# Layer 0's shift and scale taken by quarters, x transposed ahead, and the first chunk projected between the loads

## The reference, cut to what matters

```python
shift, scale, gate = split(silu(c) @ ada_w[0] + ada_b[0], 3)        # ada_w[0]: 2048 x 6144; the same for c_ctx
h  = rmsnorm(x,   norm_w[0]) * (1 + scale)   + shift                # 256 x 2048
hc = rmsnorm(ctx, norm_w[0]) * (1 + scale_c) + shift_c
q, k, v, g = split(t @ gla_w_in)                 # t = h and hc; gla_w_in: 2048 x 6144
log_a[d] = log_sigmoid((t @ gate_a1[d]) @ gate_a2[d] + gate_b[d]) / 16      # d = 0, 1; rank 16
```

## Time and profile before

| | |
|---|---|
| median of the runs | 1828.95 us |
| span of the profiled execution | 1822.9 us |
| what lies around it, from the median | 6.0 us |
| TensorE busy | 1711.7 us, 94% |
| VectorE / ScalarE busy | 908.2 us (50%) / 553.2 us (30%) |
| DMA | 265.54 MB, mean 146 GB/s |

### The profile page before, as it was taken

One profiled execution on the slowest core, in us unless ns is written; L12 is line 12 of the kernel. 1 busy time (PEld: TensorE's weight loads), 2 busy tenths in 40 slices (PEclk: granted clock), 3 DMA queues, 4 the chain that ended last, 5 costly groups with the idle time before them and its releaser, 6 DMA issues.

```text
span 1822.9 us, 19640 instructions
## 1 busy us (share of the span) xinstructions
PE 1711.7 (94%) x7996; PEld 1276.2 (70%) x7996; DVE 908.2 (50%) x1523; ACT 553.2 (30%) x805; POOL 2.2 (0%) x9
## 2 busy tenths in 40 slices
PE   3869999999999999989999799999999999997798
PEld 0237687778678777857777577877787787776476
DVE  0126544354353426455333457575565756557564
ACT  1222333233333323333222323242332323233142
POOL 0000000000000000000000000000000000000000
PEclk9579999999999999999999899999999999999799
DMA  8975422453344245223555326244433524423063
GB/s 316 386 279 174 146 86 73 160 173 93 105 154 141 88 144 178 83 81 130 194 173 190 115 78 224 93 139 136 153 127 116 185 81 133 158 93 124 14 194 118
DMA packets 185582, 265.54 MB, mean 146 GB/s; under 512 B 16090, under 2 KB 99988, under 8 KB 184980
## 3 DMA queue, kind: packets, MB, share of 16 engines
q1 hardware_dynamic: 180660, 256.68, 42.8%
q10 hardware_dynamic: 4832, 7.60, 1.4%
HBM read 262.14 MB, written 2.10 MB: 145 GB/s over the span
## 4 chain that ended last, share of the span: by engine, by line
PE 86%; DVE 5%; DMA 4%; SPq 2%; ACT 1%; issue 1%; ACTq 0%; DVEq 0%
PE bank L716 70%; PE bank L677 4%; DMA w_raw<-in_ada_w 4%; PE bank L838 2%; PE bank L787 2%; PE bank L930 2%; PE bank L914 2%; PE bank L735 1%; SPq L317 1%; PE bank L783 1%; DVE w_lo L971 1%; PE bank L685 1%; ACT w_hi L434 1%; DVE work L1251 1%; DVE work L1054 1%
## 5 line engine op out<-in xcount | busy, mean ns | idle before, releaser
L716 PE MATMUL bank<-w_lo,acts_hi 128*128 128x512 f32 x1664 | 667.1, 401 | 15.1 <-DVE acts_lo L1077 7.2
L716 PE MATMUL bank<-w_hi,acts_lo 128*128 128x512 f32 x1664 | 649.8, 391 | 0.0
L716 PE MATMUL bank<-w_hi,acts_hi 128*128 128x512 f32 x1664 | 649.5, 390 | 0.0
L971 DVE TENSOR_TENSOR w_lo<-w_raw,w_hi 128x1024 fp32r<-128x1024 f32 x288 | 351.6, 1223 | 478.6 <-ACT w_hi L434 478.4
L434 ACT ACTIVATE w_hi<-w_raw 128x1024 fp32r<-128x1024 f32 x288 | 303.9, 1058 | 897.0 <-PE bank L716 877.0
L716 PEld LDWEIGHTS bank<-w_lo,acts_hi 128*128 128x128 f32 x1664 | 313.1, 188 | 126.8 <-issue 38.2
L716 PEld LDWEIGHTS bank<-w_hi,acts_lo 128*128 128x128 f32 x1664 | 313.0, 188 | 67.1
L716 PEld LDWEIGHTS bank<-w_hi,acts_hi 128*128 128x128 f32 x1664 | 313.5, 188 | 62.4 <-issue 1.7
L677 PE MATMUL bank<-ada_w,silu_p 128*32 128x512 f32 x640 | 98.8, 693 | 24.3 <-DMA ada_w<-in_ada_w 24.3
L716 PE MATMUL bank<-acts_hi,w_lo 128*128 128x512 f32 x256 | 104.1, 407 | 10.3 <-DVE acts_lo L1077 10.3
L716 PE MATMUL bank<-acts_lo,w_hi 128*128 128x512 f32 x256 | 100.3, 392 | 0.0
(11 more groups left out here) (150 smaller groups left out, 1181.5 us busy)
## 6 DMA issues: line engine op xcount, KB each, us to landing
ada_w<-in_ada_w SPq DMA_DIRECT2D x80, 1024.0 KB, 7.6
w_raw<-in_diff_w_in SPq DMA_DIRECT2D x256, 256.0 KB, 3.0
w_raw<-in_gla_w_in SPq DMA_DIRECT2D x192, 256.0 KB, 3.0
w_raw<-in_ada_w SPq DMA_DIRECT2D x16, 1024.0 KB, 9.2
w_raw<-in_gla_w_out SPq DMA_DIRECT2D x64, 256.0 KB, 3.4
w_raw<-in_diff_w_out SPq DMA_DIRECT2D x64, 256.0 KB, 3.5
u<-in_x SPq DMA_DIRECT2D x2, 1024.0 KB, 13.9
u<-in_ctx SPq DMA_DIRECT2D x2, 1024.0 KB, 16.5
```

Of the source, the lines that this page charges most:

```text
L716: last = pe.matmul(bank[t][:], a, b, start=(k == 0 and i == 0), stop=(k == NK - 1 and i == 2))
L971: dve.tensor_tensor(w_lo[:, p % RING], raw[:, p % RING], w_hi[:, p % RING].bitcast(F32), ALU.subtract)\
```

## The change

**Loads.** x and ctx are issued first, the vectors, constants and `gate_a1` from ScalarE's queue, the last in one transfer with 8 KB rows, which TensorE turns by 16 small transposes. The startup quads come in the order shift 0, scale 0, shift 1, scale 1 and so on (`startup_chunk`), so that each group of eight completes four k-tiles. Quads 0 to 7 use three slots; from quad 8 on there are six, four of them in the space of x and ctx, so quads 8 to 11 wait for the last transpose (`xt_ok`). The pairs of chunk 0 are loaded two with each group of eight quads.

**x ahead.** Squares, norm and the 16 transposes come before modulation: VectorE copies the even transposed tiles out of their bank, ScalarE the odd, to `xT` in SBUF.

**By quarters.** With each two blocks taken, VectorE scales and shifts four k-tiles of `xT` in place, ScalarE rounds them, VectorE takes the remainders. TensorE projects two pairs of chunk 0 and 8 of the gate columns' 32 matmuls (four k-tiles) for each quarter, between the quads of the next.

**Background quads.** None is left in chunk 0: the first four go behind pairs 8 to 11, the next behind 21 to 24, the next behind 26 to 29 (before: 0, 1, 3, 5; 7, 8, 10, 11; 24, 25, 27, 29).

The core of the diff, without the empty lines, the new names of semaphores and the moved small loads:

```diff
     i, q = m // 4, m % 4
+    if i < 3:
+        return ((8, 9, 10, 11), (21, 22, 23, 24), (26, 27, 28, 29))[i][q]
     if i < 2 * G_HEADS:
         return 3 * (i // 2) * PAIRS + ((7, 8, 10, 11) if i % 2 else (0, 1, 3, 5))[q]
     if i < 2 * G_HEADS + 4:
         return (OUT0 + i - 2 * G_HEADS) * PAIRS + (0, 1, 3, 5)[q]
     return (DIFF + 4 * (i - 2 * G_HEADS - 4)) * PAIRS + (5, 7, PAIRS + 2, PAIRS + 5)[q]
+def startup_chunk(i):
+    return i // 2 + 4 * (i % 2)
+def startup_slot(n):
+    if n < 8:
+        return n % 3, n // 3
+    r, s = (n - 8) // 6, (n - 8) % 6
+    return (3 + s, r) if s < 4 else (s - 4, 3 + r)
+ADA_USES = 7
...
+        xT = view(0, NK, TOK)
+        x_sq = view(0, NT, D)
+        a1_raw = work[0:2 * NK, NT * D:NT * D + P * G_RANK].rearrange("e (p r) -> e p r", r=G_RANK)
...
-        quad_slot = [ada_w[:, 0], ada_w[:, 1], raw_quads[:, 0:4], raw_quads[:, 4:8]]
-        vec1 = view(9728, P)
-        vec2 = view(9856, P)
-        lam_pr = view(9984, 2)
+        u_quads = u[:].rearrange("p t (j n) -> p t j n", n=CW)
+        quad_slot = [ada_w[:, 0], ada_w[:, 1], raw_quads[:, 4:8]] + [u_quads[:, t] for t in range(NT)]
...
             def startup_quad(n):
-                if n >= 4:
-                    sp.wait_ge(ada_used, n - 3)
-                a, q = n // 4, n % 4
-                sp.dma_start(quad_slot[n % 4], aw0[:, 4 * q:4 * q + 4, a * CW:(a + 1) * CW]).then_inc(ada_in[n % 4], 16)
+                slot, _ = startup_slot(n)
+                if 3 <= n < 8:
+                    sp.wait_ge(ada_used, n - 2)
+                elif 8 <= n < 12:
+                    sp.wait_ge(xt_ok, NK)
+                elif n >= 12:
+                    sp.wait_ge(ada_used, n - 5)
+                a, q = startup_chunk(n // 4), n % 4
+                sp.dma_start(quad_slot[slot], aw0[:, 4 * q:4 * q + 4, a * CW:(a + 1) * CW]).then_inc(ada_in[slot], 16)
...
+            def first_chunk(q):
+                late = q == 3
+                for n in range(8 * q, 8 * q + (7 if late else 6)):
+                    startup_quad(n)
+                load_pair(0, 2 * q, q_and_k(0))
+                for n in range(8 * q + (7 if late else 6), 8 * q + 8):
+                    startup_quad(n)
+                load_pair(0, 2 * q + 1, q_and_k(0))
+            for q in range(4):
+                first_chunk(q)
...
+            def columns_out(ks):
+                for k in ks:
+                    act.wait_ge(xt_ok, k + 1)
+                    act.activation(xT[:, k], bank[5][:], ACT.Copy).then_inc(xT_odd, 1)
+            row_squares()
+            rsqrt(1, NT)
+            act.wait_ge(sq_ok, NT)
+            columns_out((1, 3))
             modulation_rows(0)
-            act.wait_ge(a1_in, 32)
-            act.activation(a1[:, NK], a1_raw[:, 0:2], ACT.Copy)
-            act.activation(a1[:, 0:NK, 0], a1_raw, ACT.Copy).then_inc(a1_hi_ok, 1)
-            modulation_rows(1)
-            act.wait_ge(x_in, 16 * NT)
-            row_squares()
-            modulation_rows(2)
-            rsqrt(1, NT)
-            for a in range(3, STARTUP):
-                modulation_rows(a)
-            splits(0, range(4))
-            high_parts(0, hf, 0)
+            columns_out(range(5, NK, 2))
+            act.wait_ge(a1_t, 1)
+            act.activation(a1[:, NK], ones[:, 0:4 * G_RANK].rearrange("p (a r) -> p a r", a=2), ACT.Copy)
+            act.activation(a1[:, 0:NK, 0].rearrange("p k (d r) -> p k d r", d=2),
+                           bank[5][:].rearrange("p (r d k) -> p k d r", r=G_RANK, d=2), ACT.Copy).then_inc(a1_hi_ok, 1)
+            for q in range(4):
+                if q > 0:
+                    modulation_rows(2 * q)
+                modulation_rows(2 * q + 1)
+                split(0, 2 * q)
+                for k in range(4 * q, 4 * q + 4):
+                    act.wait_ge(hf_ok, k + 1)
+                    act.activation(hi[:, k, :], xT[:, k], ACT.Copy).then_inc(hi_ok, 1)
+                    if k % 4 == 1:
+                        split(0, 2 * q + 1)
...
-                pe.wait_ge(ada_in[slot], 16 * (n // 4 + 1) if n < QUADS else 16 * (STARTUP + (n - QUADS) // 2 + 1))
+                pe.wait_ge(ada_in[slot], 16 * (1 + (startup_slot(n)[1] if n < QUADS else ADA_USES + (n - QUADS) // 2)))
+                if n == QUADS + 4:
+                    pe.wait_ge(d2_ok, 1)
...
+            def startup_quads(first, last):
+                for n in range(first, last):
+                    ada_quad(n, startup_slot(n)[0], bank[6 + n // 4 % 2])
+            def startup_sum(i):
+                modulation_sum(i, bank[6 + i % 2])
+            def row_transposes(k0):
+                for k in range(k0, k0 + 4):
+                    if k > 1:
+                        pe.wait_ge((xT_even, xT_odd)[k % 2], k // 2)
+                    for t in range(NT):
+                        last = pe.transpose(bank[4 + k % 2][:, t * P:(t + 1) * P], u[:, t, k * P:(k + 1) * P], ident[:])
+                    last.then_inc(xt_ok, 1)
+            def gate_weight_transposes():
+                pe.wait_ge(a1_in, 16)
+                pe.wait_ge(xT_odd, NK // 2)
+                for r in range(G_RANK):
+                    last = pe.transpose(bank[5][:, r * 2 * NK:(r + 1) * 2 * NK], a1_raw[:, :, r],
+                                        ident[0:2 * NK, 0:2 * NK])
+                last.then_inc(a1_t, 1)
+            def first_pair(p):
+                pe.wait_ge(acts_ok, 2 * p + 2)
+                project_pair(0, p, NT, False)
+            def gate_columns(q):
+                if q == 0:
+                    pe.wait_ge(a1_ok, 1)
+                    pe.wait_ge(xT_even, NK // 2)
                 columns = a1[:].rearrange("p k a r -> p (k a r)")
-                for k in range(NK):
+                for k in range(4 * q, 4 * q + 4):
                     w = columns[:, k * 4 * G_RANK:k * 4 * G_RANK + P]
                     pe.matmul(bank[4][:], w, hi[:, k, :], start=(k == 0), stop=False)
                     last = pe.matmul(bank[4][:], w, lo[:, k, :], start=False, stop=(k == NK - 1))
-                last.then_inc(z_ok, 1)
-                pe.wait_ge(zT_ok, 1)
+                if q == 3:
+                    last.then_inc(z_ok, 1)
+                    pe.wait_ge(zT_ok, 1)
+            startup_quads(0, 4)
+            pe.wait_ge(xn_ok, NT)
+            row_transposes(0)
+            startup_quads(4, 5)
+            startup_sum(0)
+            row_transposes(4)
+            startup_quads(5, 6)
+            row_transposes(8)
+            startup_quads(6, 7)
+            row_transposes(12)
+            gate_weight_transposes()
+            startup_quads(7, 9)
+            startup_sum(1)
+            for q in range(3):
+                n = 8 * (q + 1)
+                startup_quads(n + 1, n + 2)
+                first_pair(2 * q)
+                startup_quads(n + 2, n + 4)
+                first_pair(2 * q + 1)
+                startup_quads(n + 4, n + 5)
+                startup_sum(2 * q + 2)
+                gate_columns(q)
+                startup_quads(n + 5, min(n + 9, QUADS))
+                startup_sum(2 * q + 3)
+            first_pair(6)
+            first_pair(7)
+            gate_columns(3)
...
-            gla_head(0, before=transposing(0, xn), gates=gate_columns)
-            for h in range(1, G_HEADS):
+            for h in range(G_HEADS):
...
-            take_modulation(0, 0, 0, bank[6])
-            dve.wait_ge(a1_hi_ok, 1)
-            dve.tensor_tensor(a1[:, 0:NK, 1], a1_raw, a1[:, 0:NK, 0].bitcast(F32), ALU.subtract).then_inc(a1_ok, 1)
-            take_modulation(1, 0, 4, bank[7])
             dve.wait_ge(sq_ok, NT)
             inverse_rms(1, NT, D)
-            row_norm(range(NT))
-            for a in range(2, STARTUP):
-                take_modulation(a, 0, 4 * a, bank[6 + a % 2])
-            scale_columns(0, STARTUP)
...
-            dve.wait_ge(xn_ok, NT)
-            activation_tiles(0, hf, modulated(0), 0)
+            def columns_out(ks):
+                for k in ks:
+                    dve.wait_ge(xt_ok, k + 1)
+                    dve.tensor_copy(xT[:, k], bank[4][:]).then_inc(xT_even, 1)
+            def first_remainder(k):
+                dve.wait_ge(hi_ok, k + 1)
+                dve.tensor_tensor(lo[:, k, :], xT[:, k], hi[:, k, :].bitcast(F32), ALU.subtract).then_inc(acts_ok, 1)
+            def first_quarter(q):
+                for i in (2 * q, 2 * q + 1):
+                    a = startup_chunk(i)
+                    take_modulation(i, 0, 4 * a, bank[6 + i % 2])
+                dve.wait_ge(ada_taken, 2 * q + 2)
+                s = mod[:, 1, 4 * q:4 * q + 4]
+                w = cols1[:, V_NORM + 4 * q:V_NORM + 4 * q + 4].unsqueeze(2).broadcast_to([P, 4, 2])
+                st.step(dve.scalar_tensor_tensor(s, s, 1.0, w, ALU.add, ALU.mult))
+                st.wait()
+                emit = modulated(0)
+                for k in range(4 * q, 4 * q + 4):
+                    dve.wait_ge((xT_even, xT_odd)[k % 2], k // 2 + 1)
```

(72 more changed lines are left out.)

99 lines of the change are left out of this document (45 added, 54 removed).

## The result

The changed kernel took 1811.05 us (median of 4 runs, 1809.72 to 1813.36) against 1827.11 (4 runs) of the kernel before beside it: ratio 0.9914, 95% interval 0.9893 to 0.9935. It is faster by 16.1 us, where 27.1 were forecast; the time is 9.2 us above the forecast and inside the range. The profiled span went from 1822.9 to 1807.9 us, 15.0 less.

What follows compares the result with a forecast made beforehand. DMA was taken to bound the first stretch (quad loads), PE the last. 190.64 - 155.2 - 5.8 - 2.5 = 27.1 us gained: span 1795.8, with 6.0 added time 1801.9 us; range 1786 to 1819.

Steps and rivals of the forecast that it cites:

- The bound: Start of the old kernel: DMA bounds the quad loads, PE the work after; moving that work into the loads gains time.
- the mark: End of chunk 0's gate columns (start of the first gate_zT copy): 190.64 us before, forecast 155.2, 35.4 earlier.
- Term 1, DMA: Loads before the mark: 40 quads' worth at 2.71 us, 108.4 us of a full queue, with DMA running ahead of PE.
- The first rival: In the quarters DMA is the bound at 24.4 us each; gain 41.5 us, time 1787.4; chance 0.17.
- Term 2, the start: From the launch through norm, transposes and first quads: last transpose at about 45, sum 1 ends at 53.9 us.
- all at the fast rate 47.7: Lower bound for the end of sum 1 if all PE work in the start runs at the fast rate: 47.7 us.
- The fourth rival: The start takes longer through the held quads, sum 1 at 58.7 or later: gain 22 or less, 1807; no separate chance.
- Term 3, a quarter: Each quarter after an odd sum: PE's serial list with a 4.8 us chain, 27.6 us against DMA's 24.4; last quarter 18.8.
- pair 6.7: First pair of each quarter, behind a 3.8 us PE pause: starts slow and takes 6.7 us, against 5.5 at speed.
- No loss of clock: PE holds the fast level through the pause, first pairs take 5.5 instead of 6.7: the time 5 us less.
- The two rivals in which the clock stayed low for quads and small matmuls too: In the quarters: partly low, 1823 (half of that 1812), chance 0.20; low throughout, 1834.4, chance 0.06 with the like.
- Term 4, given back: Behind the mark: 5.8 us for moved background quads and a sum, 2.5 us waiting for a quad after pair 10.

Runs made afterwards that it cites:

- gates_last: Changed kernel with all 32 gate-column matmuls behind pair 7 of chunk 0 instead of a quarter at a time; ratio 0.9902 to the kernel before, 1812.01 us.
- three_quads: Changed kernel with all three free quads of a quarter put into the pause before its first pair, instead of one; ratio 0.9862 to the kernel before, 1801.57 us.
- transposes_together: all_five with all 16 transposes in one run behind quad 4, so quads 8 to 11 are issued sooner; ratio 0.9764 to the kernel before, 1783.00 us.
- all_five: Changed kernel with squares_first, pair_11, three_quads and remainder_first together, plus 15 filler matmuls in the last quarter's pause; ratio 0.9777, 1785.62 us.
- squares_first: Changed kernel with ACT's row squares ahead of its SiLU, which waits for a constant; ratio 0.9868 to the kernel before, 1803.36 us.
- remainder_first: Changed kernel with each quarter's first weight remainder made while the sum still runs, not between the tiles; ratio 0.9875 to the kernel before, 1807.28 us.
- busy_fit: Changed kernel with 6, 15, 15 and 20 useless PE matmuls filling the pauses before the four first pairs; ratio 0.9858 to the kernel before, 1799.28 us.
- pair_11: Changed kernel with the third background quad of chunk 1 one pair later, behind pair 11; ratio 0.9887 to the kernel before, 1808.61 us.
- busy_pause: Changed kernel with 12, 26, 26 and 32 useless PE matmuls in the pauses before the four first pairs; ratio 0.9885 to the kernel before, 1808.31 us.

## Why the prediction was right, and by how much it was not

**The bound (right).** DMA bounded the old start and PE did too little beside it; the change took 25.9 us off the mark. In the kernel before, 65.3 us of PE's work (125.34 to 190.64) followed the loads; now 14.9 us follow the last pause (149.88 to 164.78). No run takes the parts of the change apart, so how much each gave is not shown. Of one part the traces give a size: the gate weights, in pieces of 16 floats, kept the 16 DMA engines as full as large loads do but at half the rate in 28 to 33 us of the kernel before (first line); the kernel after moved large loads there (second line). That is 5 x (1 - 187 / 376) = 2.5 us of load, by estimate, and that is no large share of the 25.9.

```profile
28.00:33.00 5.00, 0.00 (x0) 0.00 (x0) 0.00 (x0) 0.78 (x2) 0.00 (x0) 1.00 1.01 187
```

```profile
28.00:33.00 5.00, 0.85 (x4) 0.00 (x0) 4.65 (x8) 0.18 (x1) 0.00 (x0) 1.00 1.06 376
```

**Term 1, DMA (right).** 40 quads' worth could run ahead of PE: in the changed kernel PE waited 0.6 us for DMA in 30 to 160 us, and gates_last lengthened sum 1 to mark by 1.5 us, not 5.5. The first rival (1787.4) did not come; but it stood only some 3 us a quarter away, as 27.6 against 24.4 says: three_quads waits for DMA in each of its first three quarters, and transposes_together runs two of them in 24.4 and 24.5.

**Term 2, the start (mis-sized: 53.9, measured 58.3).** The step that failed is "ACT's 13 small issues [...] hold ACT until about 6.5, hidden: it would only wait for x". Their issue was hidden; their landing wasn't. The squares stood behind SiLU in ACT's order, and SiLU behind a constant that landed at 17.3, so that they began at 19.84 and not at 11 to 12. The landing of the constants issued on ACT's queue (line 477) in the kernel after (before, line 282: 1.8 to 1.9 us):

```profile
DMA to landing us min/median/max: 9.4/10.0/11.2
```

The last transpose ended at 49.3 for 45; with the squares first, sum 1 was at 53.55, which is the forecast's 53.9. Part of that hit is luck. In squares_first the transposes began at 29.08, behind quad 3, and not at 27; they and the quads between them then took 15.3 us and not 17.7, as most of them ran at the fast pace (a quad 1.00, a sum 1.05) where the slow one was priced (1.76, 1.80). (The lower bound "all at the fast rate 47.7" comes out at 48.8 by its own terms, four quads at 1.0 and two sums at 0.8; nothing rests on it.) The fourth rival, a longer start with sum 1 at 58.7, so came in its number (58.3), but not through the held quads that it named. The held quads idled DMA as forecast: a share of 0.37 over 13 us (37 to 50) is 8.2 us without load, for 7. In the changed kernel that cost PE little, as it had other work until 53.9 and waited 0.6 us; in the versions that DMA bounds it is a price in full: transposes_together issues them 4.0 us sooner than all_five and has the mark 4.2 sooner.

**Term 3, a quarter (the order right, one price off).** The chain came out at 4.8 us exactly (87.47 to 92.29), by luck, as errors cancel: a tile took 0.65 to 0.73, not 0.5, but the takes cost 0.4 and not 0.6, and a remainder 0.60 in the chain and not 0.68. Behind it 4 quads took 3.57, not 4.0. What was mis-sized is the first pair ("pair 6.7"): 8.30, 7.36 and 8.56. The row of 7.08 that I leaned on was behind a longer pause, and I took the shorter to cost less. The runs don't show that: behind 10.3 us of idle the row was 7.08, behind 3.0 and 3.9 (the changed kernel) 8.30, 7.36 and 8.56, behind 2.0 and 2.9 (remainder_first) still 7.70, 7.36 and 7.35. Behind one and the same pause of 3.9 us it was 7.1 to 8.6 over the kernels. busy_fit measured the price with everything else in place: 1.6 to 2.8 us a quarter. No loss of clock, which I had priced at 5 us, is worth 8.1 to 9.0.

For the clock the row was 1.93 against 1.07 for a quad. The pairs now show it too: 8.30 us at a granted clock of 0.67, begun slow and ended fast, against 5.73 at 1.00 behind fillers. The Trainium skill ("TensorE: Matmul & The Clock Gate", "What's actually happening") says that the lower clock is the default and that activity lifts it. By that rule matmuls of no use in a pause should pay, and busy_fit agrees, with 8.1 to 9.0 us.

The two rivals in which the clock stayed low for quads and small matmuls too (1812 to 1823, and 1834.4) did not come: in the quarters quads took 0.9 to 1.0 and sums 0.98 to 1.07, but for the quad right behind sum 1 (1.93), which the chain through DVE covers. Their near end, 1812, lies by the measured time, but by other terms.

**Term 4, given back (mis-sized: 8.3, measured 12.6).** The wait for the quad behind pair 10 came where it was put, at 2.95 us for 2.5. It also cost some 1.7 us of slower work behind it, which was not in the sum at all, though the same price stood in term 3. Of the other 2.6 the wait's own length is 0.45 and 0.2 could not be placed. From chunk 1's pair 13 to the gate logits of head 1 it was 5.6 us more for 4 quads and a sum, which I had at 4.8: a pair behind a quad took 5.67, not 5.45. Some 1.1 us lie further on and were not traced to a place.

**The sum of the misses** at layer 1's norm is 4.4 + 4.3 + 0.9 + 4.3 = 13.9 us, less 1.7 that the rest ran faster: the span is 12.1 above the forecast 1795.8. That the time is only 9.2 above its forecast is luck: the 6.0 us added to the span were 3.1 in the changed kernel (1811.05 less 1807.9). What stays open: why the constants land so late. They are issued at 4.6 to 6.6 us, while x, ctx and the first quads fill the 16 engines (a DMA share of 1.04 in 3 to 8 us, against 0.35 in the kernel before); that those hold them up was not tried by itself.

## To carry to other kernels

When work is moved beside a stream of loads, write PE's program out as a serial list per stage and look for the spot where it waits for another engine: what stands there decides, and independent work of the same length belongs exactly in that spot. Price a pause of PE at its length plus what the matmuls behind it lose by the clock (here 1.6 to 2.8 us on 3 to 5 us, and still 1.6 to 2.0 on 2 to 3 us), and if there is no work for it, matmuls of no use that end just before the pause does are better than nothing, while ones that outlast it give the gain back. A small load that has moved behind large ones must be priced by its landing, and everything queued behind its waiter with it.

## What the runs showed of the hardware

- Loads of 1 to 64 KB, issued on ACT's queue while x and 1 MiB quads were in flight on SyncE's, landed after 9.4 to 11.2 us; the same constants took 1.8 to 1.9 us in the kernel before, where nothing large was in flight. The cause is not shown.
- The granted clock in the first pair behind a pause of 2.0 to 3.9 us was 0.64 to 0.80 (7.1 to 8.6 us); behind the same pause filled with matmuls of no use up to its last 0.3 to 0.9 us it was 1.00 (5.7 to 5.8 us).
- A wait of 0.6 us in a stretch that ran fast left the quad behind it at 1.07 us and its pair undisturbed (pair_11); one of 1.71 us already cost clock (three_quads, 0.87 over the next 48 matmuls), and one of 2.95 us made quad and pair 1.72 and 6.63.
- A matmul of 128 x 128 by 128 f32 columns took 0.23 us at the full clock (26 in 6.00 us at 1.00, recorded as 52, busy_pause), as long as one of the gate columns' matmuls of 512 columns in the rounded type.
- The same stretch of 780 us, from layer 1's norm to the end, took 781.4 to 787.7 us over kernels that don't differ in it.
